# A ring of 17 pairs of expert weight tiles in place of 12, with x stored in DRAM during the experts

## The reference

```python
g_logits = hf @ w_group + b_group            # 4 groups, top 1
e_logits = hf @ w_router + b_router          # 32 experts, top 2 in the group
...
hu = xb @ w13[e]                             # w13: 32 x 1024 x 1024
a_, b_ = split(hu)
y = (silu(a_) * b_) @ w2[e]                  # w2: 32 x 512 x 1024
...
x = x + g2 * sum over the two experts of y * gate
return rms_norm(x) * final_norm_w
```

## Time and profile before

| | before |
|---|---|
| median of 3 runs | 2707.59 us (2703.14 to 2710.5) |
| profiled execution, its own time | 2708.65 us |
| its span | 2706.6 us |
| PE busy | 2237.9 us, 83% |
| DVE busy | 1327.2 us, 49% |
| ACT busy | 789.8 us, 29% |
| POOL busy | 617.5 us, 23% |
| mean granted TensorE clock | 0.878 |
| DMA in all | 349.39 MB |
| weight loads to `raw` | 192 of 1024 KB |

### The profile page before, as it was taken

How to read it: one execution, slowest core, us unless ns; L and a number is a source line. 1 busy time by engine, 2 the same in 40 slices (tenths; PEclk the granted TensorE clock), 3 DMA queues, 4 the chain that set the end, 5 groups by cost and what they waited for, 6 DMA issues and landing times. The chain is left out here.

```text
span 2706.6 us, 43728 instructions
## 1 busy us (share of the span) xinstructions
PE 2237.9 (83%) x15715; PEld 1667.7 (62%) x15715; DVE 1327.2 (49%) x1458; ACT 789.8 (29%) x1044; POOL 617.5 (23%) x468
## 2 busy tenths in 40 slices
PE   2699978677635697798962298998999999999998
PEld 1588857456622354454531286676888888888887
DVE  7666365623533576687868601775342212221334
ACT  3221122210122576676751201553110000000113
POOL 0133223131220000000012231322333333333334
PEclk6799966779566898899985699899999999999999
DMA  6333210022459987789933010000111111111113
GB/s 257 130 116 116 80 64 0 1 113 84 178 217 419 372 346 274 316 319 392 364 130 108 16 47 19 1 0 32 54 47 46 47 47 51 49 47 47 47 51 120
DMA packets 100278, 349.39 MB, mean 129 GB/s; under 512 B 8285, under 2 KB 18935, under 8 KB 99975
## 3 DMA queue, kind: packets, MB, share of 16 engines
q1 hardware_dynamic: 83543, 314.17, 30.6%
q0 software_dynamic: 5984, 19.93, 2.2%
q10 hardware_dynamic: 10704, 14.68, 1.5%
HBM read 321.47 MB, written 27.28 MB: 129 GB/s over the span
## 5 line engine op out<-in xcount | busy, mean ns | idle before, releaser
L1443 PE MATMUL moe_hu<-moe_wup,moe_xt 128*32 128x256 f32 x5120 | 339.6, 409 | 73.6 <-DVE moe_xt L1379 39.7
L1362 DVE COPY moe_wup<-moew_raw 128x2048 f32 x243 | 269.7, 1135 | 183.4 <-DMA moew_raw<-in_w 141.5
L1443 PEld LDWEIGHTS moe_hu<-moe_wup,moe_xt 128*32 128x32 f32 x5120 | 163.6, 116 | 203.5 <-issue 70.3
L237 PE MATMUL ff_acc<-ff_yh,ff_w_hi 128*128 128x512 f32 x704 | 274.4, 390 | 0.0
L237 PE MATMUL ff_acc<-ff_yl,ff_w_hi 128*128 128x512 f32 x704 | 273.9, 389 | 0.0
L237 PE MATMUL ff_acc<-ff_yh,ff_w_lo 128*128 128x512 f32 x704 | 273.9, 389 | 0.0
L1362 ACT ACTIVATE moe_wup<-moew_raw 128x2048 f32 (+1 forms) x121 | 197.3, 1630 | 121.8 <-DMA moew_raw<-in_w 92.6
L205 POOL CAST ff_w_hi<-ff_w_raw 128x1024 fp32r<-128x1024 f32 (+1 forms) x82 | 82.0, 1000 | 545.5 <-PE ff_acc L237 545.5
L237 PE MATMUL ff_acc<-xh,ff_w_hi 128*128 128x512 f32 x480 | 188.2, 392 | 8.0 <-DVE ff_w_lo L221 7.3
L207 POOL TENSOR_TENSOR ff_w_lo<-ff_w_raw,ff_w_hi 128x1024 fp32r<-128x1024 f32 (+1 forms) x82 | 188.8, 2303 | 6.6
L237 PE MATMUL in_acc<-xh_mix,in_w_hi 128*128 128x512 f32 x368 | 144.3, 392 | 55.2 <-DVE in_w_lo L221 55.2
(11 more groups left out here) (335 smaller groups left out, 3924.3 us busy)
## 6 DMA issues: line engine op xcount, KB each, us to landing
moew_raw<-in_w SPq DMA_DIRECT2D x192, 1024.0 KB, 17.2
ff_w_raw<-in_w_up SPq DMA_DIRECT2D x44, 512.0 KB, 3.2
in_w_raw<-in_w_in SPq DMA_DIRECT2D x23, 512.0 KB, 3.3
x_res<-in_w_ada SPq DMA_DIRECT2D x20, 512.0 KB, 5.1
y_scratch<-moe_ysb ACTq DMA_DIRECT2D x80, 128.0 KB
prep_wa<-in_w_ada SPq DMA_DIRECT2D x18, 512.0 KB, 6.0
ff_w_raw<-in_w_down SPq DMA_DIRECT2D x16, 512.0 KB, 3.3
qkv_w_raw<-in_w_qkv SPq DMA_DIRECT2D x12, 512.0 KB, 3.4
```

The lines of the kernel that those rows point to most:

```text
L237: m = pe.matmul(o, w[:, b, k * P:(k + 1) * P], x[:, k, h:h + HALF], start=(k == 0 and t == 0), stop=(k == kt - 1 and t == 2))
L1362: m = e.activation(to, src, ACT.Copy) if k == "act" else e.tensor_copy(to, src)
L1443: m = e.matmul(hu[u % 2][rows(j), 0:2 * FW].rearrange("p (a f) -> p a f", a=2), xt[:, t, rows(u)], w[:, :, FW * j:FW * (j + 1)], start=(t ...
```

## The change

`raw` becomes a ring of 17 pairs (2.83 experts). Pair p of expert x lies at place (6x + p) mod 17, and takes the place of the pair that was loaded 17 pairs earlier: pair p+1 of expert x-3, or for p = 5 pair 0 of expert x-2. The room comes from three sources. x is written to DRAM ahead of the first loads in `route` and read back by SP at the end of `moe`, and its memory serves as `wup`. The memory of `acc_sq` serves as `ysb`. In `route` some small tables lie in `hst`, and one table of 100 x 32 is computed in two halves.

```diff
-                self.raw = self.weights.sb("raw", [P, 2, UT, D])
+                self.raw = self.weights.sb("raw", [P, RING, 2 * D])
...
-                    for x in range(2):
-                        for p in range(UT // 2):
-                            if x:
-                                e.wait_ge(self.s_w[p], 16)
-                            e.dma_start(self.raw[:, x, 2 * p:2 * p + 2, :], self.expert_pair(x, p)).then_inc(self.s_w[p], 16)
+                    e.dma_start(self.xt_dram, self.x[:, :, :]).then_inc(self.s_spill, 16)
+                    for n in range(RING):
+                        o, p = n // NPAIR, n % NPAIR
+                        if o:
+                            e.wait_ge(self.s_w[p], 16 * o)
+                        e.dma_start(self.raw[:, n, :].rearrange("p (a d) -> p a d", a=2), self.expert_pair(o, p)).then_inc(self.s_w[p], 16)
...
+                    e.wait_ge(self.s_spill, 16)
                     e.wait_ge(s_scatter, 16 * 2 * NT)
...
-                    do(e.tensor_tensor(ended, over(end.unsqueeze(1), NTAB, NE), over(self.const("iotab").unsqueeze(2), NTAB, NE), ALU.is_le))
-                    do(e.tensor_reduce(expert, ended, AX.X, ALU.add))
+                    for h in range(2):
+                        ended = scratch[:, 0:H * NE].rearrange("p (v x) -> p v x", x=NE)
...
-            wup, wdown = st.sb("wup", [P, KT, D]), st.sb("wdown", [P, FF // P, D])
+            wup, wdown = self.x, st.sb("wdown", [P, FF // P, D])
...
-            ysb = st.sb("ysb", [P, CT, YW])
+            ysb = self.acc_sq[:, :].rearrange("p (u c) -> p u c", u=CT)
...
-            landed = lambda o, t, n: raw[:, bass.ds(o % 2, 1), t:t + n, :].rearrange("p a t d -> p (a t d)")
+            place = lambda o, p: (NPAIR * o + p) % RING
+            landed = lambda o, t, n: raw[:, bass.ds(place(o, t // 2), 1), D * (t % 2):D * (t % 2 + n)].rearrange("p a d -> p (a d)")
...
+                    def load(x, p, was, gone):
+
+                        e.wait_ge(s_copied[was], 2 * gone)
+                        e.nop(nofuse=True)
+                        e.wait_ge(s_w[p], 16 * x)
+                        at = place(x, p)
...
+                    load(2, NPAIR - 1, 0, ended(0))
+                    with e.Fori(0, NE - 3) as i:
+                        gone = ended(i)
+                        for p in range(NPAIR - 1):
+                            load(i + 3, p, p + 1, gone)
+                        load(i + 3, NPAIR - 1, 0, ended(i + 1))
+                    n = ngroups(e)
+                    for p in range(KT // 2):
+                        e.wait_ge(s_copied[p], 2 * CT * n + 2 * (CT + 1))
+                    e.wait_ge(s_upfree, KT * CT * n + KT * (CT + 1))
+                    e.dma_start(self.x[:, :, :], self.xt_dram).then_inc(self.s_spill, 16)
...
                     mix(0, 0, 32)
+                    e.wait_ge(self.s_spill, 32)
                     body(0, 0, True)
```

More of the change, by code:

```diff
@@ L41 @@
 UT = KT + FF // P
+NPAIR, RING = UT // 2, 17
 FW, YW = FF // CT, D // CT
@@ L288, in build @@
             with self.stage("moew") as self.weights:
-                self.raw = self.weights.sb("raw", [P, 2, UT, D])
+                self.raw = self.weights.sb("raw", [P, RING, 2 * D])
+                self.s_spill = self.weights.sem("spill")
                 self.s_w = [self.weights.sem(f"w{p}") for p in range(UT // 2)]
@@ L1117, in route @@
             table = st.sb("table", [NGRP + 2, P])
-            W = {}
+            scratch = hst[:, :, :].rearrange("p b n -> p (b n)")
+            W, at = {}, 1600
+            for name, n in (("before_tile", NT * NE), ("cnt", NE), ("nb", NE), ("run0", NE), ("run1", NE), ("start", NE)):
+                W[name] = scratch[:, at:at + n]
+                at += n
             def buf(name, *shape):
@@ L1283, in _ @@
                     do(e.tensor_tensor(rank, total[:, 0:NT * NE].rearrange("p (t x) -> p t x", x=NE), upto, ALU.add))
-                    more, nb = buf("more", NE, T // TOK), buf("nb", NE)
+                    more, nb = scratch[:, 0:NE * (T // TOK)].rearrange("p (x s) -> p x s", s=T // TOK), buf("nb", NE)
                     do(e.tensor_tensor(more, over(cnt.unsqueeze(2), NE, T // TOK), over(self.const("tok_steps").unsqueeze(1), NE, T // TOK), ALU.is_gt))
@@ L1302, in _ @@
                     do(e.tensor_copy(self.slots[:, :], buf("slot", 2 * NT)), "slots")
-                    ended, expert = buf("ended", NTAB, NE), buf("expert", NTAB)
-                    do(e.tensor_tensor(ended, over(end.unsqueeze(1), NTAB, NE), over(self.const("iotab").unsqueeze(2), NTAB, NE), ALU.is_le))
-                    do(e.tensor_reduce(expert, ended, AX.X, ALU.add))
+                    expert, H = buf("expert", NTAB), NTAB // 2
+                    for h in range(2):
+                        ended = scratch[:, 0:H * NE].rearrange("p (v x) -> p v x", x=NE)
+                        do(e.tensor_tensor(ended, over(end.unsqueeze(1), H, NE), over(self.const("iotab")[:, H * h:H * (h + 1)].unsqueeze(2), H, NE), ALU.is_le))
+                        do(e.tensor_reduce(expert[:, H * h:H * (h + 1)], ended, AX.X, ALU.add))
                     do(e.tensor_scalar(expert, expert, float(NE - 1), None, ALU.min))
@@ L1327, in experts @@
         raw, s_w = self.raw, self.s_w
-        UPP, NPAIR = KT // 2, UT // 2
         UP_DVE = (((0, 2), (4, 2), (6, 2)), ((0, 2), (4, 2), (6, 1)))
@@ L1383, in _, with ended @@
                 def _(e):
[L1384 to L1391, removed]
+                    def load(x, p, was, gone):
[3 more added lines that the diff above has]
+                        at = place(x, p)
+                        dst = raw[:, at, :] if isinstance(at, int) else raw[:, bass.ds(at, 1), :].rearrange("p o d -> p (o d)")
+                        e.dma_start(dst.rearrange("p (a d) -> p a d", a=2), self.expert_pair(x, p)).then_inc(s_w[p], 16)
+                    def ended(x):
+                        return e.value_load(self.end_of[0:1, x:x + 1] if isinstance(x, int) else self.end_of[0:1, bass.ds(x, 1)], min_val=1, max_val=NTAB)
+                    load(2, NPAIR - 1, 0, ended(0))
[9 more added lines that the diff above has]
+                    e.dma_start(self.x[:, :, :], self.xt_dram).then_inc(self.s_spill, 16)
                 @blk.gpsimd
```

## The result

| | us |
|---|---|
| before, median of 9 runs | 2707.2 (2703.14 to 2710.65) |
| changed, median of 9 runs | 2716.18 (2713.21 to 2719.31) |
| ratio | 1.0034, 95% interval 1.0023 to 1.0044 |
| spans of the two profiled executions | 2706.6 and 2715.8 |

The account below looks back on a forecast made before the run. In moe, engines and weight loads were taken to bound in turn; in route, PE's loop. -32 (moe) + 21 (route) + 1 (reading x back) = -10 us gave 2698 us, with 8 in 10 from 2682 to 2716.

Parts of the forecast that it names:

- The pause cost 2.8 us at least; I take 3.5: In moe, at 970 to 990 and near 1215: more room removes two short queue pauses, 3.5 us gained each.
- a lead, once won, is kept: In moe: gains at the start, the pauses and expert 16 add up, 12.5 + 3.5 + 12.5 + 3.5 = 32 us.
- head start: Start of moe: with seventeen pairs there instead of twelve, every later load lands five loads earlier, 12.5 us gained.
- -32: Whole moe stage: sum of the gains from more room, 32 us, bounds 25 and 40.
- The place behind expert 16: In moe: five more loads fill the ring in idle time at expert 16, saving 12.5 of 21.1 us of waits.
- `route`: 21 forecast: In route: the write of x and five loads ahead of the first htok write delay rows by 21 us, 18 to 24.
- No cost from places and addresses: In moe: x as wup, acc_sq as ysb and ring addresses cost nothing, or up to 4 us.
- The reading back: End of moe: reading x back may disturb the last y_scratch write, 0 to 3 us, taken as 1.
- A: Rival, moe: all idle DMA share before a wait is usable, gain 45 to 53 us, time 2677 to 2685; chance 0.15.
- B: Rival, moe: only the first 12.5 us are gained, ring places being freed too late; time 2717; chance 0.13.
- D: Rival: reading x back shows or the copies slow down, 4 to 14 us more, 2702 to 2712; chance 0.12.
- C: Rival, route: the htok writes are not held up, -32 + 1 gives 2677; chance 0.05.

Follow-up runs that it names:

- ring12: The changed kernel with a ring of 12 pairs instead of 17, x still written to DRAM and read back; 2719.6 us.
- a_e2: The changed kernel with each y_scratch write described as 2 x 64 rows, 2 rows apart in DRAM (comb gathers other rows' values); 2845.4 us.
- a_y16: The changed kernel (17 pairs) with each y_scratch write as 128 rows of 1 KB in one dimension (comb gathers other rows' values); 2654.8 us.
- y4: The changed kernel with the write of x and five added loads behind the htok writes, and each y_scratch write issued as four of 32 rows; 2636.8 us.
- b_y16: The kernel before (12 pairs) with each y_scratch write as 128 rows of 1 KB in one dimension (comb gathers other rows' values); 2669.1 us.
- b_y4: The kernel before (12 pairs, x not moved) with each y_scratch write issued as four of 32 rows; 2681.7 us.
- late_x8: The kernel of late, reading back only an eighth of x at the end of moe (part of the computation left out); 2690.9 us.
- late: The changed kernel with the write of x and the five added loads issued behind the htok writes in route; 2694.2 us.

## Why the prediction was wrong

**The account of the four engines.** From a chain of loads without a pause one can fit what each kind of work costs the engines that carry y: 2.46 us for a load, 1.47 for a unit's y (32 packets of 46 ns, the packets' median in the trace), 1.3 for a gather (8 packets of some 160 ns). Counting the packets of y's and gathers that started between two landings (in all 73.2 y's and 19 gathers before, 73.6 and 20 in the changed kernel; the other gathers came before load 18), the remainder is idle time:

| loads | before: us, idle | changed: us, idle |
|---|---|---|
| 18 to 22 | 10.0, -0.5 | 15.1, 4.0 |
| 22 to 78 | 164.8, -0.1 | 166.4, 0.8 |
| 78 to 90 (pause at 989) | 42.1, 0.8 | 41.4, 0.8 |
| 90 to 102 | 37.0, -0.3 | 39.1, 1.2 |
| 102 to 114 (expert 16) | 71.5, 21.8 | 55.3, 10.0 |
| 114 to 138 | 74.9, 0.4 | 78.6, 0.1 |
| 138 to 150 (pause at 1215) | 41.0, -0.4 | 43.2, 3.1 |
| 150 to 191 | 137.5, -0.9 | 141.5, 0.9 |
| whole | 578.8, 20.8 | 580.7, 20.9 |

A row is good to about 1 us: those of `ring12`, which has the loads and the room of the kernel before, differ from its rows by up to 1.2. The same costs, with 5.9 / n us for a y on n engines, leave 23 us idle in `a_e2`, 21 in `a_e8`, 23 in `a_y16` and 25 in `y4`, but 53 in `b_y16` and 63 in `b_y4`. The costs are fitted to these traces, so the account is a description, not a proof; that it holds for writes on 2, 8 and 16 engines, which it wasn't fitted to, is what speaks for it.

**The step that failed: "The pause cost 2.8 us at least; I take 3.5", twice.** I compared the landing before and after a pause with 2.50 us, the time of a load in a full queue. But in the pause the four engines wrote y's and gathered x, which they would otherwise have done between the loads. Over loads 78 to 90 and 138 to 150, where the two pauses lie, their idle time before was 0.8 and -0.4 us: there was nothing to win. With the pauses gone these loads took 0.7 us less and 2.2 us more.

**The second step that failed: that a lead, once won, is kept.** Here is how far the changed kernel's units are ahead, by their down copies counted from 0, with `route`'s 20.6 us taken off: 12.4 us at unit 24, 9.6 at unit 30 (forecast 16), 21.1 at unit 42 (forecast 28.5), 15.6 at the last (forecast 32). So the head start came out, the stretch with the first pause lost 2.8 instead of gaining 3.5, expert 16 gave 11.5 for 12.5, and what follows lost 5.5 instead of gaining 3.5. Of the 16.4 us between -32 and -15.6 the two pause terms are 7; the rest is, but for 1 us, lead that was given back. Where weights come earlier, units finish earlier and their y's fall among the loads. Loads 114 to 150 met 15.6 y's before and 16.9 after, and 0.6 gathers more, 2.7 us of work; some 3.3 us of idle time came on top, whose cause stays open. Loads 150 to 191 took 4.0 us longer, with 1.6 y's more (2.4 us) and 1.8 us of idle time. The start gave 4.0 us of new idle time too: room was full before the first unit had freed a place. It didn't cost the head start.

**What was right.** The head start: 12.5 forecast, loads 22 to 60 are 12 us ahead. The place behind expert 16: 12.5 forecast, the units behind it went from 9.5 to 21 ahead. `route`: 21 forecast, 20.6 measured, `rows` at 788.7 where 789 was forecast, the first write issued at 704.5 (704) and ACT's wait 28.15 (29). No cost from places and addresses: `ring12`. Within the 21 the shares were off: the write of x alone gave about 7, not 8.7 (`ring12`), and the loads the rest.

**The reading back** was sized at 1 with bounds of 0 to 3; it cost 4.2. By `late_x8` some 3.3 to 3.7 of it are the transfer itself.

**The rivals.** A, that the idle share is a reserve, fell: the share rose to 0.98 and the time didn't fall. B forecast 2717 and the time was 2716, but that is luck: its mechanism is not what happened, the room was filled at expert 16 and gave its 12 us. Its deciding line, less than 22 us in `moe`, was the right one. D was right in kind, with 3.2 us beyond the forecast where it had 4 to 14. C fell by the changed kernel's own trace: ACT's wait for the `htok` write grew to 28.15 us, and in `late`, without the transfers ahead of it, it is 6.58.

**The unused sentence.** I had the rule of the Trainium skill ("DMA: Bandwidth & Descriptors", "Why a DMA increments its semaphore by 16 and not by 1") in hand, that such a write lies on four engines, and used it only to say that the twelve others are no reserve. Worked through with the costs above, it says more: from load 18 on the four had some 558 of 579 us of work, so beyond the head start at most 21 us could be won, whatever the waits and pauses look like. The runs agree with the rule: 4, 2, 8 and 16 small packets per write, and loads that took 580.7, 672.0, 525.4 and 500.1 us.

## What to carry to other kernels

Before giving a queue more room, add up the work of its busiest member over the stage; a pause seen at the issuing engine is idle time only if no other work was done in it, and a shorter wait on one engine is time gained only if no other wait grows. Look at the rate in GB/s beside the share. A small write whose slowest dimension is short can be dear: 128 KB on four engines took 1.47 us of them, as much as 0.6 MB of well spread loads (2.46 us for 1 MB). Here four writes for one gave 2.1% (2694.2 to 2636.8), and only then was the room worth its 45 us. And place added transfers behind the writes that a serial loop waits for.

## What the runs showed of the hardware

- A DMA share of 0.98 with 346 GB/s, where a full queue has 1.02 with 419. In the changed kernel more load packets than before are long under way: from load 18 to 191, 2561 of 44173 took over 165 ns, against a median of 159; before 767; in `y4` 83. That they wait for the four engines is a guess, since the trace doesn't name the engine of a packet.
- The small packets of a write count its engines: 4 for 4 x 32 rows, 2 for 2 x 64, 8 for 8 x 16 apart, 16 for 128 rows, and 16 for a load.
- The packets of a `y_scratch` write behind loads start in bunches about 198 ns apart, which is close to one load packet of 159 ns and one y packet of 46: the two queues seem to take turns, packet by packet. In the changed kernel 6.2 us (median) lie between the first and the last packet of a write.
- Two dimensions that lie joined in DRAM count as one when a write is spread: 8 x 16 rows joined took 2653.1 us, with 16 small packets per write, 8 x 16 rows apart 2668.6, with 8.
- The issue of a write of 2 x 64 rows took up to 16.3 us on ACT, where its median is 1.04.
